# Four of a layer's 24 gate tiles stand between its rotations and its index heads

## The reference

```
h = x @ w_in[i]
(fq, fk, fv, ff_logit, sq, sk, sv, dq, dk, dv, iq, ik, iw, g) = split_cols(h)
log_f = log_sigmoid(ff_logit + b_forget[i])           # running sums of it bias the first 6 heads
o_fox = fox_attention(fq, fk, fv, log_f)              # 6 softmax heads
o_sb = stick_breaking_attention(sq, sk, sv)           # 5 heads, log-sigmoids instead of a softmax
dq, dk, iq, ik = rope(dq), rope(dk), rope(iq), rope(ik)
# score = sum over 8 index heads of iw * relu(iq . ik); the 64 best keys of a row are kept
o_dsa = dsa_attention(dq, dk, dv, iq, ik, iw)         # 5 softmax heads over the kept keys
gates = sigmoid(g)                                    # 3 x 1024 columns for each token
merged = gates[0]*(o_fox @ w_up_fox) + gates[1]*(o_sb @ w_up_sb) + gates[2]*(o_dsa @ w_up_dsa)
x = layer_norm(ALPHA*x + merged @ w_out)              # then an MLP and a second norm
```

## Time and profile before

| | |
|---|---|
| median of 3 runs | 1770.48 us (1767.99 to 1770.70) |
| the profiled execution | 1770.61 us, its span 1768.8 us |
| granted TensorE clock | 0.899 of full speed |
| PE busy | 1588.3 us (90%) |
| DVE busy | 960.4 us (54%) |
| ACT busy | 675.3 us (38%) |
| PE in the chain that ended last | 26% of the span; DVE 2%, ACT 1% |

### The profile page before, as it was taken

One profiled execution on the slowest core, in us unless ns is written; L12 is line 12 of the kernel. 1 busy time (PEld: TensorE's weight loads), 2 busy tenths in 40 slices (PEclk: granted clock), 3 DMA queues, 4 the chain that ended last, 5 costly groups with the idle time before them and its releaser, 6 DMA issues. The chain is left out here.

```text
span 1768.8 us, 24459 instructions
## 1 busy us (share of the span) xinstructions
PE 1588.3 (90%) x9907; PEld 1345.4 (76%) x9907; DVE 960.4 (54%) x1489; ACT 675.3 (38%) x1107; POOL 36.8 (2%) x59
## 2 busy tenths in 40 slices
PE   3898899999879998998988799997998898799996
PEld 1565788655649997897888699985996887699984
DVE  0642976433345555348557645556348557755555
ACT  2012223211224443344675244444244664244442
POOL 0001210000000000000000000000000000000000
PEclk8978889865689999898998899998898998899998
DMA  9521101132044552362222465542462222565520
GB/s 358 189 91 52 48 1 49 49 140 99 1 165 168 189 190 73 121 195 92 100 96 96 176 243 183 207 142 75 124 190 96 96 96 96 185 242 187 193 95 24
DMA packets 118806, 230.46 MB, mean 130 GB/s; under 512 B 17984, under 2 KB 32448, under 8 KB 117952
## 3 DMA queue, kind: packets, MB, share of 16 engines
q1 hardware_dynamic: 115696, 221.37, 35.8%
q10 hardware_dynamic: 3024, 7.90, 1.2%
HBM read 228.21 MB, written 1.05 MB: 130 GB/s over the span
## 5 line engine op out<-in xcount | busy, mean ns | idle before, releaser
L706 DVE TENSOR_TENSOR work_rounded<-ring,work_rounded 128x1024 fp32r<-128x1024 f32 x208 | 240.9, 1220 | 114.5 <-ACT work_rounded L698 114.4
L669 PE MATMUL psum<-channels_rounded,work_rounded 128*128 128x256 f32 x2048 | 285.1, 286 | 0.7 <-DVE work_rounded L736 0.7
L669 PEld LDWEIGHTS psum<-channels_rounded,work_rounded 128*128 128x128 f32 x2048 | 271.1, 195 | 4.7 <-issue 3.3
L680 PE MATMUL psum<-work_rounded 128*128 128x512 f32 x1152 | 265.7, 390 | 0.0
L922 PE MATMUL psum<-channels_rounded,ring_rounded 128*128 128x256 f32 x1728 | 252.0, 289 | 3.0 <-DVE channels_rounded L1351 3.0
L698 ACT ACTIVATE work_rounded<-ring 128x1024 fp32r<-128x1024 f32 x208 | 203.2, 1049 | 132.7 <-PE psum L680 118.5
L680 PEld LDWEIGHTS psum<-work_rounded 128*128 128x128 f32 x1152 | 214.8, 188 | 43.6
L922 PEld LDWEIGHTS psum<-channels_rounded,ring_rounded 128*128 128x128 f32 x1728 | 228.6, 197 | 5.3 <-DVE channels_rounded L1351 3.8
L1343 DVE TENSOR_TENSOR ring_rounded<-ring,ring_rounded 128x1024 fp32r<-128x1024 f32 x80 | 94.5, 1195 | 64.6 <-ACT ring_rounded L1166 64.4
L746 DVE TENSOR_TENSOR work<-work 128x512 f32<-128x512 f32 x48 | 33.2, 692 | 108.9 <-ACT work L718 108.9
L1166 ACT ACTIVATE ring_rounded<-ring 128x1024 fp32r<-128x1024 f32 x80 | 80.6, 1025 | 27.5 <-DMA ring<-in_w_in 27.5
(11 more groups left out here) (361 smaller groups left out, 2313.3 us busy)
## 6 DMA issues: line engine op xcount, KB each, us to landing
ring<-in_w_in SPq DMA_DIRECT2D x20, 2048.0 KB, 7.9
ring<-in_w_ff SPq DMA_DIRECT2D x16, 2048.0 KB, 7.5
ring<-in_w_ff_in SPq DMA_DIRECT2D x16, 2048.0 KB, 8.4
ring<-in_w_ff_out SPq DMA_DIRECT2D x16, 2048.0 KB, 7.8
ring<-in_w_mod SPq DMA_DIRECT2D x12, 2048.0 KB, 8.0
ring<-in_w_out SPq DMA_DIRECT2D x6, 2048.0 KB, 7.8
ring<-in_w_in SPq DMA_DIRECT2D x8, 1024.0 KB, 5.6
ring<-in_w_up SPq DMA_DIRECT2D x4, 2048.0 KB, 8.4
```

Of the source, the lines that this page charges most:

```text
L669: mm = pe.matmul(psum[:, 4 + 2 * half + q, i * SEQ:(i + 1) * SEQ], w1[pw][:, k, m * P:(m + 1) * P], y[py][:, k, :], start=((k, n) == (0, 0 ...
L680: mm = pe.matmul(psum[:, 2 * t + n, :], h[ph][:, kq, t * P:(t + 1) * P], w2[pw][:, kq, n * 512:(n + 1) * 512], start=False, stop=False, sk ...
L706: dve.tensor_tensor(parts.low[i % 2][:, at], ring[:, SLOT * s + 1024 * c:SLOT * s + 1024 * (c + 1)], exact(parts.high[i % 2][:, at]), ALU. ...
```

## The change

In both layers the steps before the first head get a list of their own, `index_schedule`, in which four gate tiles, 0 to 3, and their DVE step "sigmoid" stand among rotations, running sums and index heads; the sums come after the second rotation instead of after the fifth. Each engine walks this list, then the heads' list without index heads. ACT does the closing exp of the four tiles behind the last index head. `gates_of` deals the other 20 tiles: one for each head, two for heads 3, 7, 11 and 15. The list of jobs, and so the banks, follows the same order. The products, splits and sums themselves are as before.

```diff
+EARLY_GATES = 4
+
+
 def gates_of(turn):
-    first = 3 * turn // 2 + turn % 2
-    return range(first, min(first + 2 - turn % 2, GATE_JOBS))
+    count = lambda n: EARLY_GATES + n + n // 4
+    return range(count(turn), min(count(turn + 1), GATE_JOBS))
+
+
+def index_schedule():
+
+    return [("rot", "ik"), ("rot", "iq01"), ("cum", ""), ("gate", "0"), ("cumT", ""), ("gate", "1"), ("sigmoid", "0"),
+            ("rot", "iq23"), ("idx", "0"), ("idx", "1"), ("sigmoid", "1"), ("gate", "2"), ("idx", "2"), ("idx", "3"),
+            ("rot", "dq01"), ("sigmoid", "2"), ("gate", "3"), ("rot", "dq4dk"), ("idx", "4"), ("idx", "5"),
+            ("sigmoid", "3"), ("idx", "6"), ("idx", "7")]
 
 
 def attention_schedule():
 
-
-
-    steps = [("idx", str(h)) for h in range(8)]
+    steps = []
...
+    for kind, n in index_schedule() + attention_schedule():
+        if kind in ("cum", "cumT"):
+            j.add(kind, "dve" if kind == "cum" else "act")
+        elif kind == "rot":
+            j.add(f"rot_{n}", "dve")
+        elif kind != "sigmoid":
...
+                        def gate(n):
+                            w.done(channels(w.open(f"gate_{n}"), 0, unit(f"g{n // 4}", n % 4 + 1), (n % 4) * P))
...
+                        for kind, name in index_schedule():
+                            if kind == "rot":
+                                rotation(name)
+                            elif kind == "gate":
+                                gate(int(name))
+                            elif kind == "idx":
+                                index_scores(int(name))
+                            elif kind == "cum":
+                                ps = w.open("cum")
+                                pe.wait_ge(lf_ready, 1)
+                                pe.matmul(ps[:, 0:6], const_a("upto"), lf3[:, 0:6], start=True, stop=True)
+                                pe.matmul(ps[:, 6:12], const_a("upto"), lf3[:, 6:12], start=True, stop=False)
+                                w.done(pe.matmul(ps[:, 6:12], const_a("ones"), lf3[:, 0:6], start=False, stop=True))
+                            elif kind == "cumT":
+                                ps = w.open("cumT")
+                                w.after("cum")
+                                for t in range(TT):
+                                    mm = pe.transpose(ps[0:6, t * P:(t + 1) * P], cneg[:, 6 * t:6 * t + 6], ident)
+                                w.done(mm)
...
+                        def sigmoid_start(n):
+                            act.wait_ge(products_done, j2.full(f"gate_{n}"))
+                            g = sig[:, SEQ * n:SEQ * (n + 1)]
+                            step(act.activation(g, psum[:, j2.bank(f"gate_{n}"), 0:SEQ], ACT.Abs))
+                            step.wait()
+                            step(act.activation(g, g, ACT.Exp, scale=-1.0))
+                            step.wait()
+                            act.activation(g, g, ACT.Ln, bias=1.0).then_inc(gate_ln, 1)
+                            high(f"g{n // 4 + 1}" if n < 20 else "up0", (n % 4,), f"gate_{n}")
...
+                        for kind, name in index_schedule():
+                            if kind == "cumT":
+                                ps = r.open("cumT", 256)
+                                r.read("cumT", act.activation(cT[0:6, :], ps[0:6, :], ACT.Copy))
+                            elif kind == "idx":
                                 h = int(name)
                                 if h >= 2:
                                     act.wait_ge(idx_used, h - 1)
                                 r.read(f"idx_{name}", act.activation(rl[h % 2], r.open(f"idx_{name}", 384), ACT.Relu))
                             elif kind == "gate":
+                                sigmoid_start(int(name))
+                        for n in range(EARLY_GATES):
+                            sigmoid_end(n)
...
+                        def next_low(n):
+                            if n >= 4:
+                                low(f"g{n // 4}" if n < 24 else "up0", n % 4)
+
+                        def sigmoid(n):
+                            g = sig[:, SEQ * n:SEQ * (n + 1)]
+                            dve.wait_ge(gate_ln, n + 1)
+                            dve.scalar_tensor_tensor(out=g, in0=psum[:, j2.bank(f"gate_{n}"), 0:SEQ], scalar=0.0,
+                                                     in1=g, op0=ALU.min, op1=ALU.subtract).then_inc(emptied["gate"], 1)
+
...
+                        for kind, name in index_schedule():
+                            if kind == "rot":
+                                rope(f"rot_{name}", rotated[name])
+                            elif kind == "cum":
+                                r.read("cum", dve.tensor_scalar(cneg, r.open("cum", 12), -8.0, None, ALU.mult))
+                            elif kind == "sigmoid":
+                                sigmoid(int(name))
+                                next_low(int(name) + 3)
+                            elif kind == "idx":
+                                index_sum(int(name))
```

More of the change, by code:

```diff
@@ L988, in _, with rotation @@
                         hi64, all128 = slice(HD, P), slice(0, P)
[L989 to L992, removed]
+                        rotated = {"ik": ((0, ikT, all128),), "iq01": ((0, iqT[:, 0:512], all128),),
+                                   "iq23": ((0, iqT[:, 512:1024], all128),), "dq01": ((0, dqT[:, 0:512], all128),),
+                                   "dq4dk": ((0, dqT[:, 512:768], hi64), (256, dkT, all128))}
+                        def rotation(name):
                             ps = w.open(f"rot_{name}")
                             w.after({"ik": "ikw", "dq4dk": "dk"}.get(name, name))
-                            for at, src, rows in parts:
+                            for at, src, rows in rotated[name]:
                                 n = src.shape[-1]
@@ L998, in _ @@
                             w.done(mm)
[L1000 to L1006, removed]
@@ L1026, in _ @@
                                 continue
+                            if kind == "gate":
+                                gate(int(name))
+                                continue
                             ps = w.open(f"{kind}_{name}")
[L1028 to L1040, removed]
+                            if kind == "S":
                                 if name == "fox0":
@@ L1230, in _ @@
                             elif kind == "gate":
[L1231 to L1239, removed]
+                                sigmoid_start(int(name))
+                        for n in range(EARLY_GATES):
+                            sigmoid_end(n)
+                        for kind, name in attention_schedule():
+                            if kind == "gate":
+                                sigmoid_start(int(name))
                             elif kind == "S":
@@ L1396, in _ @@
                         every, hi64 = slice(0, P), slice(HD, P)
[L1397 to L1402, removed]
+                        rotated = {"ik": [(0, ikT, every)], "iq01": [(0, iqT[:, 0:512], every)],
+                                   "iq23": [(0, iqT[:, 512:1024], every)], "dq01": [(0, dqT[:, 0:512], every)],
+                                   "dq4dk": [(0, dqT[:, 512:768], hi64), (256, dkT, every)]}
@@ L1414, in _ @@
                         for kind, name in attention_schedule():
[L1415 to L1434, removed]
-                            elif kind == "sigmoid":
[L1436 to L1441, removed]
+                            if kind == "gate":
+                                next_low(int(name) + 3)
+                            elif kind == "sigmoid":
+                                sigmoid(int(name))
                             elif kind == "S":
```

38 lines of the change are left out of this document (24 added, 14 removed).

## The result

The changed kernel takes 1791.95 us (median of 4, 1783.69 to 1795.34) against 1769.27 us for the kernel before in the same comparison: ratio 1.0121, interval 1.0084 to 1.0158. It is slower by 22.7 us; 1789.0 was forecast. The profiled execution took 1795.3 us, the longest of the four, its span 1793.5.

A forecast was written before the change was run, and what follows sets the result against it. PE was taken to wait on DVE, mainly for stick-breaking weights (14.6 us) and the sums' copy (12.0 us). 1770.6 + 2 x (17.0 - 10.0) + clock 2 x 2.2 = 1789.0 us, range 1782 to 1797.

The forecast's parts named there:

- The mechanism: Index stage: gate 2, gate 3 and idx 6 wait for banks that DVE's late sigmoid steps free; 3.1, 4.9, 3.6 us.
- The loads: SP's loads behind the last tile of a unit: none needed sooner by more than one head; zero.
- The index stage without the clock: From first rotation to first head at full clock: 33.6 us against 16.4 to 16.7 before, 17.0 us later per layer.
- The heads: The 16 heads, with four fewer gate tiles among them: 10.0 us earlier per layer, not the 11.3 of four tiles.
- The terms for heads 7 and 11: Stick-breaking head 7 and head 11 get a second tile: they gain 3.1 and 4.3 us.
- The tile of 2.8 us: PE's price of one gate tile of 24 products: two take 1344.38 to 1350.22, 2.8 us each.
- The clock: Falls behind the index stage's gaps, 1.4 us each, at most 4.2 per layer; 2.2 us per layer taken.
- the 1793 us: Whole time by the skill's rule, with all three gaps of the index stage counted as clock falls: about 1793 instead of 1789.
- That the tiles cover DVE: Index stage: no gate's bank holds PE up, first head at 22 instead of 33.6 us, 1761.8 us; chance 0.06.
- Rival (c): Gates 2, 3 and 4 all at the lower clock level, 8.4 us per layer, 1801.4 us; chance 0.10.
- Leaving out a gap (1779): Index stage: banks hold PE at only two of three places, or the second gap is short; 4.9 less per layer; chance 0.12.

The follow-up runs named there:

- first two runs of the experiments: Each on the changed kernel: early gate tiles 0 to 3 in PSUM banks of their own, 1764.99 us; separately, sigmoid steps earlier in DVE's list, 1768.34 us.
- run with filling: Changed kernel, with PE's idle time before gate 2, gate 3 and idx 6 filled by products nobody reads; 1787.14 us, ratio 1.0106 to the kernel before.
- run with banks of their own: Changed kernel, with gates 0 to 3 in PSUM banks 0 to 3, one each, outside the turn of four; 1764.99 us, ratio 0.9961 to the kernel before.
- run with all of it together: Changed kernel plus early gates in banks 0 to 3, sigmoid 2 behind rotation dq4dk, splits behind V, two tiles in heads 7 to 10; 1768.05 us.

## Why the prediction was right, and where it was not

**The mechanism** held: three waits per layer for DVE's sigmoid step in front of gate 2, gate 3 and idx 6, forecast 3.1, 4.9 and 3.6 us, measured 3.0, 4.7 and 3.7. The first two runs of the experiments show that it is the banks together with DVE's order. The loads, priced at zero, brought no new wait of PE. The nearness of the whole, 1789.0 against 1791.95, is in part luck, as the terms show.

**The index stage without the clock** was mis-sized by 1.6: the prediction had the first head at 33.6, and with the clock kept up it came at 32.0. Gate 2 started at 12.7, not 13.8: rotation iq23 came at 7.8 instead of 8.4, and the two index heads behind it took PE 0.9 us, not 1.2, since the 0.62 for a head was taken from eight of them, partly spent in pacing. The last two, idx 6 and 7, took 0.8 and not 1.3.

**The heads**: 10.0 us earlier was forecast, 4.5 and 3.9 measured. The terms for heads 7 and 11 were right (11.1 against 11.2; 9.7 against 9.6, with its wait of 1.35 against 1.5). The tile of 2.8 us holds as the difference of two heads (8.78 less 5.98); the start and end that the prediction gave for it (two tiles in 5.84 us) would make it 2.9. The clock made up the rest. Head 0 took 8.9 us in layer one where the run with filling has 5.0:

```profile
837.50 0.63 PE L1049 MATMUL psum<-work 64*128 64x128 f32 x2
...
841.07 5.38 PE L931 MATMUL psum<-channels_rounded,ring_rounded 128*128 128x256 f32 x24
846.38 0.48 PE L1049 MATMUL psum<-work 64*128 64x128 f32 x2
```

Heads 8, 9 and 10 took 8.8, 7.6 and 8.6 us, together 2.4 more than the 22.6 that the same three took in layer one of the run with banks of their own. Head 12 in layer one and heads 4 and 5 in layer two were each 1.5 to 1.6 longer than at full clock. That is 7.8 and 9.4 us in the two layers. Heads of the kernel before were too long in the same way by 2.3 and 3.2 (head 4 took 10.4 us in layer one, where 8.8 is the length of two tiles at full clock). The differences, 5.5 and 6.2, are the shortfall to within 0.1 us.

**The clock** is the term that failed: 2.2 us per layer. It measured 3.6 in the stage, shown by the filled run, and 5.8 in the heads, the mean of the two shortfalls. Two steps were wrong. A fall behind a gap cost more than the 1.4 us taken from one pair of tiles: 1.5 us for gate 2, 1.5 for gate 3, and 4.5 behind the third gap, where idx 6 and 7 (1.4 us instead of 0.8), S of head 0 (3.6 instead of 2.0) and its tile all ran slowly, though index heads were said to feel the clock hardly. And every gap had its fall, not half of them; the other 1.9 us per layer were low stretches further on in the heads, which the prediction had no term for.

The sum came near by errors of opposite sign: 2 x 7.2 too little for the clock, 2 x 1.6 too much for the stage, and outside the parts that the change touches the profiled execution was 5.2 us shorter (4.1 longer ahead of layer one, 6.6 shorter between the layers' attention, 2.6 shorter behind, the last two at a clock of 0.95 instead of 0.93). 18.4 + 14.4 - 3.2 - 5.2 = 24.4 of the 24.7 us between the profiled spans.

The Trainium skill (TensorE: Matmul & The Clock Gate, "A second HAM failure mode: psum-queue depth-cycling") reports of another kernel that short pauses in turning through PSUM banks were paid for in re-warming. The low clock behind all three gaps here agrees with it; the 1793 us that the prediction reckoned by it are nearer to the measured 1791.95 than 1789.0 is, though with a clock term of 4.2 us per layer where 9.4 was measured.

**The rivals.** That the tiles cover DVE happens only when no bank ties them (own banks), and then the first head starts at 23.1, near the 22 of that rival; the time, 1765, was above its 1761.8. Rival (c) priced the clock at 8.4 us per layer, against the 9.4 measured, nearer than my forecast, but partly by luck: the three gate tiles together were 5.2 to 5.4 us too long, not 8.4, and the rest came from S, index heads and later heads. Its time of 1801.4 was too high, since it had the stage 1.6 us too long per layer and nothing for the 5.2 us that other parts came out shorter. Leaving out a gap (1779) did not happen. The running sums, the part that took away the 6.0 us wait, were worth nothing alone.

## What to carry to other kernels

Work that is moved in to cover another engine's chain should not end with a step of that same engine that stands behind the chain. Where results pass through a few banks in turn, look up for every moved job which later job gets its bank, which step frees it, and what stands ahead of that step in its engine's list; the two engines' busy times do not tell this. In a list in program order, put a step that someone waits for ahead of those nobody waits for yet, and after each such edit read the waits again, since the next queue is often the same one.

## What the hardware showed that was not expected

In the changed kernel each of the six gaps of 3 to 5 us was followed by a gate tile of 4.5 to 5.4 us where 2.8 is the full-clock time, while gaps of about 2 us between stick-breaking heads were so only at times. The length of the gap alone does not settle it: with the sigmoid steps earlier, gate 2 behind a gap of 1.65 us took its full-clock time, while in the run with all of it together head 0's tile, behind index heads, a gap of 1.4 us among them, and S, took 5.4 us in layer one. What else counts, no run here takes apart. And the kernels scatter by more than their first runs suggested: the 25 runs of the kernel before in the first comparison lay between 1748 and 1776 us, where the first three had lain within 3 us. The shortest of them had the highest mean clock, 0.920, and the longest 0.897.
